# Two more up-projection blocks as seven quarter products, with the work around them moved

## What is computed

```
def conv_ffn(h, p):
    a, b = jnp.split(h @ p["ffn_w_up"], 2, axis=-1)      # 1024 -> 2 x 2816
    a = short_conv(a, p["ffn_conv_w"], p["ffn_conv_b"])  # 3 taps along the tokens
    return (jax.nn.gelu(a, approximate=False) * b) @ p["ffn_w_down"]
```

## Time and profile before

| | |
|---|---|
| three executions | 1443.75, 1447.92, 1450.55 us (median 1447.92) |
| the profiled execution | 1448.28 us, of which the span shown by the profile 1446.6 us |
| PE busy | 1429.1 us, 99% |
| DVE, ACT, POOL busy | 873.9, 657.0, 366.8 us |
| mean granted TensorE clock | 0.997 of full |
| DMA | 243.15 MB, mean 168 GB/s |

### The profile page before, as it was taken

The page is one execution under the profiler, slowest core; times in us unless marked ns, Lnnn a source line. Parts: engine busy times, 40 slices in busy tenths (PEclk is TensorE's granted clock), DMA queues, the critical chain, the costliest instruction groups (busy, mean ns, idle before and its releaser), DMA issues.

```text
span 1446.6 us, 19430 instructions
## 1 busy us (share of the span) xinstructions
PE 1429.1 (99%) x7644; PEld 1206.5 (83%) x7644; DVE 873.9 (60%) x1321; ACT 657.0 (45%) x1048; POOL 366.8 (25%) x315
## 2 busy tenths in 40 slices
PE   9999999999999999999999999999999999999998
PEld 7777778888888888788888888888889899899987
DVE  6455766444477633565438437778757787348854
ACT  6535773233453412334336326665435565236642
POOL 1263211102032200122013422215624142124312
PEclk9999999999999999999999999999999999999999
DMA  8351116654255599656935458854653455345531
GB/s 269 122 170 63 59 44 215 211 167 148 101 200 169 173 292 280 206 182 190 302 109 184 155 188 213 216 198 146 218 160 105 144 177 173 102 130 176 179 128 59
DMA packets 72740, 243.15 MB, mean 168 GB/s; under 512 B 8455, under 2 KB 9384, under 8 KB 67658
## 3 DMA queue, kind: packets, MB, share of 16 engines
q1 hardware_dynamic: 61274, 181.22, 38.3%
q0 software_dynamic: 9744, 55.05, 13.5%
q10 hardware_dynamic: 1632, 5.64, 1.0%
HBM read 229.28 MB, written 50.35 MB: 193 GB/s over the span
## 4 chain that ended last, share of the span: by engine, by line
PE 88%; DVE 4%; DMA 4%; ACT 3%; issue 1%; POOL 0%; SPq 0%; ACTq 0%; DVEq 0%
PE PS L536 86%; DMA raw<-in_ws 3%; PE PS L549 2%; DVE wl L2043 1%; ACT wh L1356 1%; DVE TMP L2708 1%; DVE TMP L2091 0%; DMA X<-in_x 0%; ACT th L1934 0%; ACT HTh L1378 0%; DVE HTl L2059 0%; DVE tl L2718 0%; DVE TMP L2553 0%; DVE TMP L2514 0%; DVE TMP L2714 0%
## 5 line engine op out<-in xcount | busy, mean ns | idle before, releaser
L2043 DVE TENSOR_TENSOR wl<-raw,wh 128x1024 fp32r<-128x1024 f32 x222 | 299.0, 1351 | 302.6 <-ACT wh L1356 302.3
L1356 ACT ACTIVATE wh<-raw 128x1024 fp32r<-128x1024 f32 x255 | 266.7, 1054 | 236.8 <-PE PS L536 144.1
L536 PE MATMUL PS<-HTh,wh 128*128 128x512 f32 (+1 forms) x944 | 348.3, 370 | 3.8 <-DVE wl L2043 2.8
L536 PE MATMUL PS<-HTl,wh 128*128 128x512 f32 (+1 forms) x944 | 345.3, 367 | 0.0
L536 PE MATMUL PS<-HTh,wl 128*128 128x512 f32 (+1 forms) x944 | 341.2, 367 | 0.0
L536 PEld LDWEIGHTS PS<-HTh,wh 128*128 128x128 f32 x944 | 178.7, 189 | 39.3 <-issue 11.4
L536 PEld LDWEIGHTS PS<-HTl,wh 128*128 128x128 f32 x944 | 178.8, 189 | 27.3 <-DVE HTl L2059 0.7
L536 PEld LDWEIGHTS PS<-HTh,wl 128*128 128x128 f32 x944 | 176.4, 189 | 29.5 <-DVE wl L2043 0.2
L536 PE MATMUL PS<-wh,FFh 128*128 128x512 f32 (+1 forms) x442 | 170.0, 385 | 0.1
L536 PE MATMUL PS<-wl,FFh 128*128 128x512 f32 (+1 forms) x442 | 169.9, 384 | 0.0
L536 PE MATMUL PS<-wh,FFl 128*128 128x512 f32 (+1 forms) x442 | 169.8, 384 | 0.0
(11 more groups left out here) (359 smaller groups left out, 2328.7 us busy)
## 6 DMA issues: line engine op xcount, KB each, us to landing
raw<-in_ws SPq DMA_DIRECT2D x232, 512.0 KB, 4.6
raw<-sums SPq DMA_DIRECT2D x72, 256.0 KB, 2.9
sums<-in_up POOLq DMA_DIRECT2D x6, 2560.0 KB, 21.1
raw<-in_up SPq DMA_DIRECT2D x54, 256.0 KB, 3.0
sums<-in_up POOLq DMA_DIRECT2D x6, 2048.0 KB, 18.0
sums<-sums POOLq DMA_DIRECT2D x2, 2560.0 KB, 12.9
taps<-TMP SPq DMA_DIRECT2D x16, 256.0 KB, 2.4
tab<-in_spec POOLq DMA_DIRECT2D x8, 512.0 KB, 5.8
```

The costliest lines, as they stand in the source:

```text
L536: return nc.tensor.matmul(out, l, r, start=start, stop=stop, skip_group_check=True)
L1356: act(WH[u % SLOTS][:, :n], RAW[i % RAWS][:, :n], ACT.Copy).then_inc(sem("w_hi"), 1)
L2043: tt(WL[k][:, :n], RAW[RAW_AT["unit", u, 0] % RAWS][:, :n], f32(WH[k][:, :n]), ALU.subtract).then_inc(sem("lo_dve"), 1)
```

## The change

The first paired run begins at block 2 instead of block 4. Of every 7 duos GpSimd makes one low half (number 2), VectorE the other six. The eight sum DMAs of the first run are cut into two pieces of 5 blocks each (1280 KB), in strict order, each waiting for all before it: eight pieces (the two copies, the first two additions) after gated tile 15, the other eight after tiles 16, 18, ... 30. In the scalar program the turned inputs' high halves stand ahead of `gelu` of blocks 0 and 1, and the copy of the first cd stands between `gelu(1)` and `gated_high(1)`; before, it stood behind `gated_high(3)` and a weight unit. In the vector program `turned_low(0)` stands ahead of `up_gate(0)`, `turned_low(3)` behind `kernel_sum`, `turned_low(4)` in the first round of the run.

```diff
-RUNS = (range(4, 12), range(12, 22))
+RUNS = (range(2, 12), range(12, 22))
+PIECES = (2, 1)
...
-    or u in DUOS and DUOS.index(u) % 7 in (2, 5) and u not in DUOS[:3] + DUOS[28:31])]
+    or u in DUOS and DUOS.index(u) % 7 == 2 and u not in DUOS[:3] + DUOS[35:38])]
...
                     centre(m)
+                    for i in ((0, 1), (2,))[m]:
+                        turned_high(i)
+                    if m == 1:
+                        weights(duo_ahead("cd", run[0]))
                     gelu(m)
+                    if m == 1:
+                        keep_cd(run[0])
                     gated_high(m, first_m)
-                    for i in ((0, 1), (2, 3), (4,), ())[m]:
-                        turned_high(i)
-                weights(duo_ahead("cd", run[0]))
-                keep_cd(run[0])
+                if first_m:
+                    weights(duo_ahead("cd", run[0]))
+                    keep_cd(run[0])
+                else:
+                    turned_high(3)
+                    turned_high(4)
...
                     weights(unit("ffn_w_up_2", 0, 2816 + m * P) + SLOTS - 1)
+                    if m == 0:
+                        turned_low(0)
                     up_gate(m)
-                    for i in ((), (0, 1), (2, 3), (4,))[m]:
-                        turned_low(i)
+                    turned_low(m + 1)
                 weights(duo_ahead("cd", run[0]))
                 kernel_sum(run[0])
+                if first_m == 0:
+                    turned_low(3)
...
                     weights(duo_ahead("a", m - 1))
+                    if m == RUNS[0][1]:
+                        turned_low(4)
                     value_right(m - 1)
...
+            def sum_weights(n, i, after):
+
+                f, of, add = (("ac", "c", False), ("cd", "c", False), ("ac", "a", True), ("cd", "d", True),
+                              ("acd", "ac", False), ("acd", "d", True), ("abcd", "acd", False),
+                              ("abcd", "b", True))[i // PIECES[n]]
+                size = len(RUNS[n]) // PIECES[n]
+                at = PAIRED.index(RUNS[n][0]) + i % PIECES[n] * size
+                rows = slice(32 * at, 32 * (at + size))
...
+                e.wait_ge("d_sum", 16 * (8 * sum(PIECES[:n]) + after))
...
                 if q == 15:
-                    for step in range(4):
-                        sum_weights(0, step)
+                    for i in range(8):
+                        sum_weights(0, i, i)
+                if q > 15 and q % 2 == 0:
+                    sum_weights(0, q // 2, q // 2)
...
             load_tables(1, 0)
-            sum_weights(0, 4)
-            sum_weights(0, 5)
```

More of the change, by code:

```diff
@@ L2834, in load_pre @@
                 engine.dma_start(WL[k][:, :], a["wd"][i, 1]).then_inc(sem(f"d_pre{k}"), 16)
[L2836 to L2853, removed]
@@ new lines, in sum_weights @@
+            def sum_weights(n, i, after):
[5 more added lines that the diff above has]
+                rows = slice(32 * at, 32 * (at + size))
+                x = a["up4"][PLAIN.index(of), rows, :] if of in PLAIN else a["sums"][SUMMED.index(of), rows, :]
+                y = a["sums"][SUMMED.index(f), rows, :]
+                e.wait_ge("d_sum", 16 * (8 * sum(PIECES[:n]) + after))
+                if add:
+                    engine.dma_start(y, x, accum_op=ALU.add, max_dma_last_dim=8192).then_inc(sem("d_sum"), 16)
@@ L2854, in sum_weights @@
                 else:
-                    engine.dma_start(y["abcd"], x["b"], accum_op=ALU.add, max_dma_last_dim=8192).then_inc(sem("d_sum"), 16)
+                    engine.dma_start(y, x, max_dma_last_dim=8192).then_inc(sem("d_sum"), 16)
             def put_spectrum(o, part):
@@ L3003, in gpsimd_program @@
                 tt(x, x, T(r % 2), ALU.add).then_inc(sem("rp_add"), 1)
-            sum_weights(1, 0)
+            sum_weights(1, 0, 0)
+            sum_weights(1, 1, 0)
             mine = [u for u in range(PRE[2] + 1) if u > unit("w_in_2", 0, 0) and (u in POOL_LOW or u in PRE)]
@@ L3009, in gpsimd_program @@
                 weights(u)
-                if i in (0, 3, 4, 6):
-                    sum_weights(1, (0, 3, 4, 6).index(i) + 1)
+                if i == 0:
+                    sum_weights(1, 2, 2)
+                    sum_weights(1, 3, 2)
+                elif i in (3, 4, 6):
+                    n = 4 + (3, 4, 6).index(i)
+                    sum_weights(1, n, n)
             for o in range(2):
@@ L3029, in gpsimd_program @@
                     weights(unit("w_in_2", 0, 1536 + 10 * P) + SLOTS - 1)
-            sum_weights(1, 5)
+            sum_weights(1, 7, 7)
             weights(unit("w_out_2", 3 * P, 0) + SLOTS - 1)
@@ L3114, in load @@
                         if f in SUMMED:
-                            e.wait_ge("d_sum", 128 if m in RUNS[0] else 256)
+                            e.wait_ge("d_sum", 128 * (PIECES[0] if m in RUNS[0] else sum(PIECES)))
                         of, k = ("sums", SUMMED.index(f)) if f in SUMMED else ("up4", PLAIN.index(f))
```

## The result

| | before | after |
|---|---|---|
| median of 7 executions each, in turn on one chip | 1449.47 us (1443.75 to 1450.73) | 1458.59 us (1454.86 to 1459.93) |
| after / before, 95% interval | | 1.0061 [1.0044, 1.0078] |
| the profiled execution, its span | 1448.28, 1446.6 us | 1455.66, 1453.9 us |

The change makes the kernel slower by 0.61%, 9.1 us where I had summed 3.8. The median lies 1.6 us above the end of my range and over the 0.5% that I gave a chance of 0.20. The base has moved too: the kernel before has a median of 1449.47 us over seven executions, 1.6 more than the 1447.92 over three on which I built the range. As a difference, 9.1 us is just the range's upper end (1457.0 - 1447.9).

A forecast was written before the change was run, and what follows sets the result against it. The prediction took TensorE's matmul stream plus its few waits as the bound. Its terms, -4.7 - 1.6 + 6.9 + 3.2 = +3.8 on 1448.3 less 0.4, gave about 1451.7 us, range 1443.5 to 1457.0.

The forecast's parts named there:

- The other eight pieces go beside tiles 16 to 30: Second half of the first run's sum DMAs: each has two tiles (10.9 us) to land; cost 0, bound above 4.7 us.
- the old wait: TensorE's 2.8 us wait near 586 us for weights, plus slow clock behind it: taken as gone, -4.7 us, bounds -4.7 and 0.
- the starving stays: Rival, chance 0.18: wait at 586 remains or one appears among tiles 16 to 30; 1456.4 us.
- its sign: In the burst or among tiles 16 to 30, ScalarE waiting over some 15 us for a raw unit decides for that rival.
- no addition runs longer than some 11 us, less than the 15.25: In the burst after tile 15: pieces' additions stay shorter than ScalarE's 15.25 us wait that emptied the slots; wait taken as gone.
- 1.5 more: Start of the first paired run: a clock staying low over both TensorE waits would add 1.5 us; left out of the range.
- Start of the first run: At block 2, TensorE idles for the first copy (8.2 us), then for `kernel_sum`: 11.8 us lost instead of 4.9, +6.9 us.
- The start costs little: Rival, chance 0.22: VectorE gets its turn before GpSimd's queued sums at the run's start; +2.1 instead of +6.9, 1446.9 us.
- the copy really ahead of GELU: At the run's start, the first cd's copy ahead of `gelu(1)`, where the diff does not put it, would come some 3 us sooner.
- GpSimd one in seven: In 4 + 4 odd rounds of the runs, VectorE's extra low half makes TensorE wait 0.4 us each: +3.2 us, bounds 0 and 6.
- Fewer columns: Blocks 2 and 3 become paired blocks, 20.16 us instead of 21.79: gain 1.6 us.
- the pieces' side: First run's sum DMAs cut in pieces: -4.7 us for the wait near 586, cost 0 for the eight pieces beside tiles 16 to 30.

The follow-up runs named there:

- the first trace: The changed kernel's first profiled execution, nothing further changed: 1455.66 us.
- the third: The changed kernel, unaltered, profiled a third time beside two other kernels on one chip: 1460.40 us in the profiled execution, median 1458.35.
- the one-in-seven run: The kernel before with only GpSimd's share changed, to one low half in seven: median 1452.47 us, ratio 1.0027.
- the pairs of runs: Kernels differing in GpSimd's share, one or two in seven: changed kernel 1.0061 against 1.0041, late pieces 1.0034 against 0.9996, kernel before 1452.47 against 1448.43 us.

## Why the prediction was wrong in size and right in sign

**The failed step** is "The other eight pieces go beside tiles 16 to 30 ... Cost 0, bound above 4.7". I rested it on the mean share (0.58 to some 0.9; it came to 0.92) and on 10.9 us for a piece to land. The copies do land in time, the additions do not: they took 11.4, 13.7 and, the fifteenth, 17.8 us. In strict order the delay passes on, and from 643.53 on the pieces follow each other with pauses of 4.4, 2.6 and 0.3 us into the change of products. That cost TensorE 2.4 us in the first trace and 3.9 with a low clock behind it in the third; moving two pieces gave 3.9 to 5.2 us back. So the gain of the old wait (4.7) was mostly lost again 100 us later. The mechanism, weights starved by sum DMAs, was mine; that it could not strike here was wrong.

Of the rivals, *the starving stays* came nearest. It put the new wait among tiles 16 to 30; it came just behind them. Its price of 4.7 is within the 3.9 to 5.2, its 1456.4 the nearest to 1458.59. But its sign, a wait of ScalarE over some 15 us for a raw unit, never showed: the longest are 9.41 and 8.27. And the sign was no good to begin with, as a row of the kernel before tells:

```profile
549.72 1.06 ACT L1356 ACTIVATE wh<-raw 128x1024 fp32r<-128x1024 f32 x1 [16.68 <-DMA raw<-in_ws]
```

ScalarE waits 16.68 us there, longer than the 15.25 at 586 on which I built, and TensorE does not wait at all. Most likely it also counts how many units lay ready before it; no view here shows that. So "no addition runs longer than some 11 us, less than the 15.25" was no reason for the wait to go.

**The range's high end** left out a clock that stays low, "1.5 more". At the start one execution has 1.7 us more of it than another (five products in 19.5 against 17.8 us), and behind the starving it comes on top of a wait that is itself 1.5 longer. Both should have been inside. The 1.6 us by which the median lies above the range are also what the base rose by.

**The old wait gone:** right, but priced from one execution; in the one-in-seven run the same wait was 5.5 us, not 2.8. But only 1.1 of the 4.7 us were left at the first run in the profiled execution (1112.14 to 1111.09), and in the third, with acd(2) at 1115.63, nothing: it was 2.0 later than before.

**Start of the first run:** right. +6.9 forecast, +5.7 in the profiled execution (10.6 against 4.9), +7.4 in the third. Forecast were an idle of 8.2 us, then one of about 2.4; they were 7.2 and 1.6. That VectorE's instructions are stretched by turns with GpSimd's sums was shown by taking the sums away from beside the low halves; that the turns are the cost of the start was not, as the two waits then still came to 7.4 us. *The start costs little* is excluded. That the copy really ahead of GELU would come some 3 us sooner was right, and worthless: `kernel_sum` is late next.

**GpSimd one in seven:** right in place (eight waits, the first odd round of each run free) and about in size: +3.2 against 3.8 in the trace and 2.9 to 5.5 in the pairs of runs.

**Fewer columns:** -1.6, never measured by itself; the span fits: -1.1 at 1111.09, +5.7 at the start, -1.6, and +4.3 for the rest (1453.9 - 1128.90 = 325.0, against 300.6 from 1146.02 to 1446.6 before and 20.16 for two blocks more) make 7.3, which is what was found. Of the 4.3, the odd rounds are 3.8, by eight times 0.48. Set against my sum of 3.8: the pieces' side 3.6 worse (-1.1 for -4.7), the start 1.2 better, the rest 1.1 worse.

## What to carry to other kernels

Background transfers beside a stream of weights are judged neither by the mean share of the DMA engines (0.91 and 0.98 went without a wait, 0.86 came with one of 10 us) nor by the stage in which they land (two additions wholly in the next product cost nothing, eight pieces landed before it cost most). What helped in these runs was room ahead of the last additions (a share of 0.74 instead of 1.01 over 20 us); look at each piece's issue and landing, and at TensorE's waits in more than one execution. Beginning a paired, more demanding schedule earlier needs cover work on every engine that it loads: a similar reordering was worth nothing without two regular blocks ahead of it (and with GpSimd's sums beside it), and with them it took the median from 1444.26 to 1438.48. Price an idle of TensorE together with a slow clock behind it that may or may not last, and take the spread of the executions as a sign of such waits.

## What I had not expected of the hardware

The same two waits (7.2 and 1.6 us) are followed by 6.8 us of the lower clock in two executions and by 13.7 in a third. A chain of VectorE beside GpSimd's sums kept its time to the hundredth of a microsecond, 17.03, with over a microsecond of its work taken out. TensorE came through a wait of ScalarE of 16.68 us for weights without a gap, and did not through one of 8.27. One more surprise is of the profile and not of the chip: waits that the list gives as 0.2 us each come with a loss of 0.48 us each in the distance of blocks.
